# Spreading choosing steps and dense products over later stages, and moving one decoding behind a remainder, in a fused two-block layer

## The chip, the core and the metric

The kernel runs on one core of one Trainium2 chip. The metric is the device time of the whole program in microseconds (us). Five engines work side by side, each through its own program in order, and wait for each other on semaphores: TensorE (PE in the rows; PEld is its weight loads), VectorE (DVE), ScalarE (ACT), GpSimd (POOL) and SyncE (SP). GpSimd issues the gathers (indirect DMAs), SyncE the plain loads.

## The reference, cut to what matters

Two transformer blocks run one after the other on 512 tokens of width 1024. The change lies in the last part of the second, PEER: each token asks 8 heads for 16 of 16,384 single-neuron experts each, which makes 128 chosen experts for a token.

```
def peer(h, w_query, sub_keys, u_tab, v_tab):
    def block(xb):
        q = (xb @ w_query).reshape(TOKEN_BLOCK, P_HEADS, 2, P_HALF)
        s = jnp.einsum('thpk,hpnk->thpn', q, sub_keys)
        sv, si = lax.top_k(s, P_TOPK)
        cand = (sv[:, :, 0, :, None] + sv[:, :, 1, None, :]).reshape(...)
        cidx = (si[:, :, 0, :, None] * N_KEYS + si[:, :, 1, None, :]).reshape(...)
        fv, fpos = lax.top_k(cand, P_TOPK)
        eidx = jnp.take_along_axis(cidx, fpos, axis=-1)
        g = jax.nn.softmax(fv, axis=-1)
        u = u_tab[eidx]
        act = jax.nn.gelu(jnp.einsum('td,thkd->thk', xb, u), approximate=False)
        return jnp.einsum('thk,thkd->td', (g * act), v_tab[eidx])
```

The output is the sum with the residual under a last RMS norm.

## The kernel before, in words

The tokens are four blocks t = 0..3 of 128. After the dense layers of both blocks (up to about 1100 us of the span) the PEER part begins. Its query weights come as eight panels ("wq", 0..7) of 256 columns. Each panel is split into a rounded part (ScalarE, `rounded`) and a remainder (VectorE, `remainders`, L1190), and TensorE needs both before it starts on the panel (L556 to L558). Between the panels VectorE ranks one head after another of block 0 (`first_head`), and after four heads it turns places into expert numbers (`decode`, L1884 to L1919). The first 64 gathers wait for the decoding of heads 0 to 3, the other 64 for that of heads 4 to 7. A few gathered rows are used already between the panels (`FIRST_DOTS`).

Then come six stages, in the order U0, V0, U1, V1, V2, V3, each with 128 gathers of 512 KB (`gather`, L2655):

- **U0 and U1**: gather k brings, for each of the block's 128 tokens, the row of the first table that its k-th expert has, and VectorE multiplies and sums it (`dot`, L1972).
- **V0 to V3**: gather k brings the 128 rows of the second table that one token has chosen, and TensorE sums them with the weights of the token (L1145). Four tokens make one group m, so a stage has 32 groups of 16 matmul records each. ScalarE lays the weights out (`windows`, L2547). VectorE adds the result of a V stage to the residual (`finish`, L2030 to L2044).

For blocks 2 and 3 the first table is not gathered. All its 16,384 rows come as 128 plain loads of 512 KB (`ucols`, three slots, issued by SyncE as TensorE frees a slot), and TensorE multiplies each with the 256 tokens of both blocks: `dense(j)`, L1082, 16 matmul records. Afterwards 132 choosing steps `ext(s)` pick from these products those that a token has chosen: for each, TensorE spreads four tokens' key numbers (L1109, 4 records), ScalarE makes a one-hot matrix of them (L2513, L2515), TensorE multiplies with it two steps later (L1095, 8 records), and VectorE masks and sums four steps' results together (L2010, L2015, L2019). Steps 0 to 65 work on the products of the first 64 loads, steps 66 to 131 on the others. Both halves share one buffer, so dense(64) and later ones are kept only after step 65, and step 66 needs dense(127). The weights of block 2 are complete after step 99, those of block 3 after step 131.

The ranking of blocks 2, 3 and 1, in this order, is cut into 60 parts (`ranking_parts`, 20 to a block): TensorE's key scores (L1042) feed VectorE, which ranks single heads and pairs of heads and decodes twice a block. "ids" is the transposition of the expert numbers of one block (L1065, L1990).

All of this is dealt over the stages by the table `BESIDE`: an entry ("dense", 64, 124, 0, 127) means that items 64 to 123 stand evenly behind indexes 0 to 127 of the stage, an index being a gather k in a U stage and a group m in a V stage. Every engine reads the same table, so the entry sets the place of the item in each engine's program. In U1 a gather also waits for the dense products that stand 8 indexes earlier. The gathers rotate through 9 buffers in U0, 11 and then 13 from V0 on, and 17 from the 50th gather of U1 on; a gather waits until its buffer has been used.

## Time and profile before

| | us |
|---|---|
| median of 3 runs (2411.26 to 2419.2) | 2412.99 |
| profiled execution, its own time | 2416.05 |
| its span | 2414.2 |
| first gather issued | 1106.26 |
| stages by the issue of their first gather, rounded: V0, U1, V1, V2, V3 | 1370, 1591, 1825, 2017, 2211 |

Times in the rows count from the start of the span. A row of a timeline has the start, the length, engine, line, operation, output and inputs, and the count of instructions merged in it; in brackets stands the idle time before it and what ended it. A row of a window table has the window, its length, the busy time and (in brackets) the count of instructions for each engine named, then the granted TensorE clock as a share of 2.4 GHz, the mean busy share of the DMA engines, and GB/s.

### The profile page before, as it was taken

What the parts mean: (1) busy time and instruction counts of PE and PEld (TensorE: products, weight loads), DVE (VectorE), ACT (ScalarE), POOL (GpSimd) and SP (SyncE); (2) the same over time, 40 slices, a digit from 0 to 9 for tenths busy, and PEclk for the clock granted to TensorE, in tenths of its full rate; (3) what the DMA queues carried; (4) which work ended last, traced back from release to release, by engine and by line L of the source; (5) the groups of instructions that cost most, each with busy time, mean ns of one, the idle gap of its engine ahead of it and who ended that gap; (6) DMA issues with size and microseconds to landing.
All of it is one profiled execution on the core that took longest, in us unless ns stands there. A gap on an engine that the chain in (4) does not pass through costs nothing.

```text
span 2414.2 us, 31160 instructions
## 1 busy us (share of the span) xinstructions
PE 2126.6 (88%) x12429; PEld 1576.2 (65%) x12429; DVE 1308.9 (54%) x2914; ACT 643.5 (27%) x1077; POOL 885.7 (37%) x821
## 2 busy tenths in 40 slices
PE   6999889999999997899899988899898887875775
PEld 6786879889887875887788744567786454311111
DVE  3865476776456466556988775489763233100000
ACT  3335332322354333331111133421111343200000
POOL 0410000000000000002666655556766665666664
PEclk8999999999999998999999988889999898887898
DMA  4211245444212210225999998989999999999997
GB/s 178 70 36 46 112 154 198 181 174 157 89 69 105 70 53 18 88 70 185 366 415 417 406 346 312 336 309 412 413 411 419 378 343 327 348 378 368 356 374 284
DMA packets 147056, 590.01 MB, mean 244 GB/s; under 512 B 16336, under 2 KB 16464, under 8 KB 134240
## 3 DMA queue, kind: packets, MB, share of 16 engines
q0 software_dynamic: 110592, 402.70, 43.7%
q1 hardware_dynamic: 35136, 178.80, 19.7%
q10 hardware_dynamic: 1184, 6.53, 0.7%
q8 instruction: 98, 1.61, 0.3%
q14 instruction: 46, 0.38, 0.0%
HBM read 584.29 MB, written 3.67 MB: 244 GB/s over the span
## 4 chain that ended last, share of the span: by engine, by line
PE 33%; POOL 9%; DVE 8%; issue 8%; another core or an unknown queue 6%; DMA 4%; ACT 3%; SPq 0%; POOLq 0%; DVEq 0%; ACTq 0%
PE ps L1145 7%; PE ps L1082 6%; POOL big L2655 6%; PE ps L1095 5%; PE ps L556 4%; PE ps L557 4%; PE ps L558 4%; DVE cols L1972 2%; DMA big<-vtab,big 2%; DMA raw<-ucols 2%; POOL hres L2655 1%; ACT Ir L2513 1%; PE ps L1109 1%; ACT Ir L2515 1%
## 5 line engine op out<-in xcount | busy, mean ns | idle before, releaser
L1082 PE MATMUL ps<-rowb,raw 128*128 128x256 f32 x2048 | 464.4, 387 | 24.9 <-DMA raw<-ucols 22.1
L1082 PEld LDWEIGHTS ps<-rowb,raw 128*128 128x128 f32 x2048 | 391.6, 194 | 94.4 <-issue 20.8
L1145 PE MATMUL ps<-big,cols 128*32 128x512 f32 x1380 | 365.2, 692 | 77.6 <-issue 55.1
L2655 POOL DMA_INDIRECT big<-vtab,big x345 | 332.1, 963 | 190.9 <-issue 84.0
L2578 POOL TENSOR_TENSOR small<-small,cols 128x1 f32<-128x1 f32 (+3 forms) x33 | 28.9, 876 | 896.2 <-DVE small L1590 387.8
L1145 PEld LDWEIGHTS ps<-big,cols 128*32 128x32 f32 x1380 | 73.6, 121 | 254.0 <-issue 164.2
L2655 POOL DMA_INDIRECT big<-utab,cols x144 | 178.3, 1238 | 110.3 <-issue 36.6
L1972 DVE CUSTOM_DVE_ANT_0 cols<-big 128x1024 bf16<-128x1024 f32 x144 | 173.9, 1226 | 39.5 <-DMA big<-utab,cols 29.5
L1095 PE MATMUL ps<-Aj,Ir 128*128 128x64 f32 x1024 | 161.7, 301 | 27.3 <-issue 19.7
L2015 DVE TENSOR_TENSOR cols<-cols,ps 128x512 f32<-128x512 f32 x64 | 43.9, 688 | 253.0 <-remote 124.1
L2502 ACT ACTIVATE Aj<-ps 128x512 f32<-128x512 f32 x64 | 68.1, 1067 | 418.5 <-PE ps L1082 342.4
L556 PE MATMUL ps<-xhb,whb 128*128 128x512 f32 (+1 forms) x432 | 167.2, 387 | 5.9 <-ACT fbig L2356 3.0
L1095 PEld LDWEIGHTS ps<-Aj,Ir 128*128 128x128 f32 x1024 | 144.5, 214 | 38.1 <-issue 25.6
L557 PE MATMUL ps<-xhb,wlb 128*128 128x512 f32 (+1 forms) x432 | 164.1, 380 | 0.0
L558 PE MATMUL ps<-xlb,whb 128*128 128x512 f32 (+1 forms) x432 | 163.8, 379 | 0.0
L2034 DVE TENSOR_TENSOR cols<-ps,g2b 128x512 f32<-128x512 f32 x8 | 5.2, 688 | 271.3 <-remote 139.5
L2513 ACT ACTIVATE Ir<-ps,cols 128x512 f32<-128x512 f32 x128 | 87.7, 685 | 234.0 <-remote 123.8
L556 PE MATMUL ps<-whb,ah 128*128 128x256 f32 x512 | 146.0, 285 | 1.1 <-DVE al L1624 1.1
L1145 PE MATMUL ps<-hres,cols 128*32 128x512 f32 x408 | 137.1, 738 | 10.3 <-issue 5.7
L557 PE MATMUL ps<-whb,al 128*128 128x256 f32 x512 | 143.9, 281 | 0.0
L558 PE MATMUL ps<-wlb,ah 128*128 128x256 f32 x512 | 143.8, 281 | 0.0
L2109 ACT ACTIVATE whb<-raw 128x2048 fp32r<-128x2048 f32 x51 | 97.5, 1912 | 164.3 <-DMA raw<-ff 106.8
(388 smaller groups left out, 4479.7 us busy)
## 6 DMA issues: line engine op xcount, KB each, us to landing
raw<-ucols SPq DMA_DIRECT2D x128, 512.0 KB
raw<-ff SPq DMA_DIRECT2D x32, 1024.0 KB, 4.9
raw<-w SPq DMA_DIRECT2D x24, 1024.0 KB, 4.9
raw<-ada SPq DMA_DIRECT2D x24, 1024.0 KB, 4.8
raw<-wo SPq DMA_DIRECT2D x8, 1024.0 KB, 4.9
raw<-wq SPq DMA_DIRECT2D x8, 1024.0 KB, 4.8
big<-vtab,big POOLq DMA_INDIRECT x345
hres<-x SPq DMA_DIRECT2D x8, 512.0 KB, 6.4
```

What stands on the lines that cost most here:

```text
L556: e.matmul(o, lhsT=lh, rhs=rh, start=(k == 0), stop=False)
L557: e.matmul(o, lhsT=ll, rhs=rh, start=False, stop=False)
L558: ins = e.matmul(o, lhsT=lh, rhs=rl, start=False, stop=(k == n - 1))
L1082: ins = e.matmul(PS[b][:, c:c + 256], lhsT=un[j % NU][:, k, :], rhs=h2T[k // 4][:, k % 4, :], start=(k == 0), stop=(k == 7))
L1095: ins = e.matmul(PS[b][:, c:c + JC], lhsT=Ir[:, (g % 2) * 512 + q * 128:(g % 2) * 512 + (q + 1) * 128], rhs=Atd[:, 4 * g + q, :], start=Tr ...
L1145: ins = e.matmul(PS[hf][32 * j:32 * j + 32, :], lhsT=win[:, c0:c0 + 32], rhs=gs[i][:, hf * 512:(hf + 1) * 512], start=(m == 0), stop=(m == ...
L1972: e.tensor_tensor_reduce(out=junk[k % 3], in0=gs[i], in1=h2[:, t, :], scale=1.0, scalar=0.0, op0=ALU.mult, op1=ALU.add, accum_out=act[:, t ...
L2015: e.tensor_tensor(jm[n % 2], jm[n % 2], PS[(5, 7)[n % 2]][:, :], ALU.mult).then_inc(*V.mark("ex_p", (r, n)))
L2109: e.activation(hi, raw_of(n), ACT.Copy).then_inc(*A.mark("hi", u))
L2502: e.activation(Adt[:, jl:jl + 2, :], PS[2 + pair % 2][:, :].rearrange("p (j t) -> p j t", j=2), ACT.Copy).then_inc(*A.mark("dv", pair))
L2513: e.activation(one, PS[KEYS2[g % 2]][:, :], ACT.Abs, bias=pidx).then_inc(*A.mark("ex_a", r, g))
L2655: e.indirect_dma_start(gs[i], None, utab if st == "U" else vtab, bass.IndirectOffsetOnAxis(ap=idx, axis=0)).then_inc(sems[f"l_g{i}"], 16)
```

## The change

Two things are changed. In the table, the ranking of block 3 starts two heads earlier (26 parts in U0 instead of 22) and the first half of block 1's ranking ends at group 20 of V0 instead of 31. The transposition for block 2 stands behind index 126 of U0 instead of 122, and all 64 dense products of U0 stand ahead of it. The choosing steps are 50, 16, 34 and 32 in V0, U1, V1 and V2, where they were 66, 0, 54 and 12. The dense products are 64, 44 and 20 in U0, U1 and V1, where they were 64, 60 and 4.

In the panel loop, the decoding of heads 0 to 3 stands behind the remainder of panel 6 instead of ahead of it; that of heads 4 to 7 stays behind head 7.

```diff
 BESIDE = {
-    ("U", 0): [("topk", 0, 22, 10, 124), ("ids", 0, 1, 12, 12), ("ids", 1, 2, 122, 122), ("dense", 0, 64, 0, 127)],
+    ("U", 0): [("topk", 0, 26, 10, 124), ("ids", 0, 1, 12, 12), ("dense", 0, 64, 0, 125), ("ids", 1, 2, 126, 126)],
...
-    ("V", 1): [("dense", 124, 128, 0, 2), ("ext", 66, 120, 3, 31)],
+    ("V", 1): [("dense", 108, 128, 0, 11), ("ext", 66, 100, 12, 31)],
...
@@
                 if h % 2:
                     rank_pairs(0, h)
-                if h % 4 == 3:
-                    for _ in decode(0, h // 4):
-                        pass
@@
             for i in range(8):
                 panel("wq", i, last=(i == 7))
+
+                if i == 5:
+                    for _ in decode(0, 0):
+                        pass
                 if i:
                     first_head(i - 1)
...
             first_head(7)
+            for _ in decode(0, 1):
+                pass
```

The first place is VectorE's program in the panel loop. L1860 is the last operation of ranking heads 2 and 3, L1889 to L1919 are the decoding, L1190 is the remainder of panel 6, and L1844 begins head 4. Before:

```order
L1860 MAX_INDEX big<-big,cols 128x8 x2
L1889 TENSOR_SCALAR cols<-big 128x64
L1890 TENSOR_SCALAR cols<-big 128x64
L1891 TENSOR_SCALAR small<-big 128x64
L1892 TENSOR_SCALAR small<-big 128x64
L1893 TENSOR_SCALAR small<-big 128x64
L1895 COPY_PREDICATED cols<-small 128x128
```

The same place now:

```order
L1860 MAX_INDEX big<-big,cols 128x8 x2
L1190 TENSOR_TENSOR wlc<-raw,whc 128x2048
L1889 TENSOR_SCALAR cols<-big 128x64
L1890 TENSOR_SCALAR cols<-big 128x64
L1891 TENSOR_SCALAR small<-big 128x64
L1892 TENSOR_SCALAR small<-big 128x64
L1893 TENSOR_SCALAR small<-big 128x64
```

The remainder (L1190) stood behind L1919 and now stands ahead of L1889; the rest keeps its order up to head 4.

The second place is TensorE's program at the end of V0 and through U1. L1109 and L1095 are choosing steps, L1042 key scores, L1082 dense products (8 rows of this list to a product, which are 16 records of the profile), L1065 transpositions. Before:

```order
L1095 MATMUL ps<-Aj,Ir 128x64 x12
L1082 MATMUL ps<-rowb,raw 128x256 x8
L1042 MATMUL ps<-big 128x128 x2
L1082 MATMUL ps<-rowb,raw 128x256 x32
L1042 MATMUL ps<-big 128x128 x2
L1082 MATMUL ps<-rowb,raw 128x256 x24
L1042 MATMUL ps<-big 128x128 x2
L1082 MATMUL ps<-rowb,raw 128x256 x96
L1065 MATMUL ps<-cols 128x128
L1082 MATMUL ps<-rowb,raw 128x256 x320
L1065 MATMUL ps<-cols,big 128x128
```

The end of the same stretch now:

```order
L1109 MATMUL ps<-big,small 128x128 x4
L1095 MATMUL ps<-Aj,Ir 128x64 x4
L1042 MATMUL ps<-big 128x128 x2
L1109 MATMUL ps<-big,small 128x128 x4
L1095 MATMUL ps<-Aj,Ir 128x64 x4
L1109 MATMUL ps<-big,small 128x128 x4
L1095 MATMUL ps<-Aj,Ir 128x64 x12
L1082 MATMUL ps<-rowb,raw 128x256 x64
L1065 MATMUL ps<-cols 128x128
L1082 MATMUL ps<-rowb,raw 128x256 x288
L1065 MATMUL ps<-cols,big 128x128
```

The first dense product of U1 stood right behind the last choosing step of V0; now 16 choosing steps and all key scores of U1 stand ahead of it.

The third place is TensorE's program in the first groups of V1. L1145 is the weighted sum of a group. Before:

```order
L1082 MATMUL ps<-rowb,raw 128x256 x8
L1145 MATMUL ps<-big,cols 32x512 x3
L1145 MATMUL ps<-raw,cols 32x512
L1145 MATMUL ps<-big,cols 32x512 x3
L1145 MATMUL ps<-raw,cols 32x512
L1082 MATMUL ps<-rowb,raw 128x256 x16
L1145 MATMUL ps<-big,cols 32x512 x2
L1145 MATMUL ps<-B2b,cols 32x512
L1145 MATMUL ps<-big,cols 32x512 x3
L1145 MATMUL ps<-B2b,cols 32x512
L1145 MATMUL ps<-big,cols 32x512
L1109 MATMUL ps<-big,small 128x128 x4
```

The same groups now:

```order
L1082 MATMUL ps<-rowb,raw 128x256 x16
L1145 MATMUL ps<-big,cols 32x512 x3
L1145 MATMUL ps<-raw,cols 32x512
L1145 MATMUL ps<-big,cols 32x512 x3
L1145 MATMUL ps<-raw,cols 32x512
L1082 MATMUL ps<-rowb,raw 128x256 x16
L1145 MATMUL ps<-big,cols 32x512 x2
L1145 MATMUL ps<-B2b,cols 32x512
L1145 MATMUL ps<-big,cols 32x512 x3
L1145 MATMUL ps<-B2b,cols 32x512
L1145 MATMUL ps<-big,cols 32x512
L1082 MATMUL ps<-rowb,raw 128x256 x8
```

Where the choosing steps began behind the fourth group, dense products now go on, one or two behind each of the first twelve groups.

## Rows read from the trace of the kernel before

**Rows 1.** Window table of the whole core, one window a stage: PE, PEld, DVE, ACT, POOL.

```profile
1106.00:1370.00 264.00, 246.56 (x1109) 209.78 (x1109) 225.41 (x641) 33.89 (x35) 159.31 (x129) 0.97 0.94 370
1370.00:1591.00 221.00, 185.85 (x1354) 114.91 (x1357) 139.07 (x477) 89.61 (x150) 126.31 (x128) 0.86 0.89 326
1591.00:1825.00 234.00, 216.43 (x967) 181.48 (x960) 180.97 (x386) 32.40 (x33) 164.02 (x130) 0.95 1.01 405
1825.00:2017.00 192.00, 165.49 (x1136) 96.99 (x1135) 51.97 (x85) 67.85 (x115) 124.00 (x129) 0.92 0.99 374
2017.00:2211.00 194.00, 150.81 (x756) 52.20 (x758) 24.99 (x39) 26.80 (x54) 121.78 (x129) 0.83 0.94 352
2211.00:2397.00 186.00, 129.73 (x520) 29.07 (x512) 5.19 (x7) 3.25 (x15) 123.18 (x129) 0.88 0.96 367
```

**Rows 2.** Window table of L1145 alone: PE and PEld.

```profile
1370.00:1594.00 224.00, 79.54 (x512) 15.66 (x512) 0.86 0.88 322
1840.00:1868.00 28.00, 12.10 (x64) 2.39 (x64) 0.94 1.03 418
1868.00:1912.00 44.00, 18.41 (x128) 3.80 (x128) 0.92 1.00 398
1912.00:2036.00 124.00, 52.14 (x320) 11.69 (x320) 0.89 0.95 343
1496.00:1594.00 98.00, 39.18 (x256) 7.69 (x256) 0.85 0.78 278
```

**Rows 3.** Window table of L1082 alone: PE and PEld.

```profile
1106.00:1370.00 264.00, 215.96 (x960) 182.50 (x960) 0.97 0.94 370
```

**Rows 4.** Timeline of VectorE in the panel loop.

```profile
1098.34 0.20 DVE L1889 TENSOR_SCALAR cols<-big 128x64 uint32<-128x64 uint32 x1
...
1106.06 2.29 DVE L1190 TENSOR_TENSOR wlc<-raw,whc 128x2048 fp32r<-128x2048 f32 x1
...
1112.95 1.23 DVE L1972 CUSTOM_DVE_ANT_0 cols<-B2b,big 128x1024 bf16<-128x1024 f32 x1 [2.02 <-DMA B2b<-utab,cols]
...
1116.40 2.29 DVE L1190 TENSOR_TENSOR wlc<-raw,whc 128x2048 fp32r<-128x2048 f32 x1
```

**Rows 5.** Timeline of TensorE at the start of panels 5 and 6.

```profile
1091.82 0.61 PE L1042 MATMUL ps<-big 128*128 128x128 f32 x4
...
1103.40 0.61 PE L1042 MATMUL ps<-big 128*128 128x128 f32 x4
1108.50 0.76 PE L556 MATMUL ps<-xhc,whc 128*128 128x512 f32 x1 [4.50 <-DVE wlc L1190]
```

**Rows 6.** Timeline of all engines at the end of U0.

```profile
1375.04 10.53 PE L1082 MATMUL ps<-rowb,raw 128*128 128x256 f32 x48
...
1380.24 1.22 DVE L1972 CUSTOM_DVE_ANT_0 cols<-big 128x1024 bf16<-128x1024 f32 x1
...
1387.94 0.31 ACT L2557 ACTIVATE big<-big 128x128 f32<-128x128 f32 x1
```

**Rows 7.** Timeline of all engines from the end of V0 to U1.

```profile
1587.92 1.28 DVE L2015 TENSOR_TENSOR cols<-cols,ps 128x512 f32<-128x512 f32 x2
...
1591.15 1.26 POOL L2655 DMA_INDIRECT big<-utab,cols  x1 [12.07 <-DVE cols L1919]
...
1600.54 1.29 DVE L2034 TENSOR_TENSOR cols<-ps,g2b 128x512 f32<-128x512 f32 x2
...
1604.69 1.23 DVE L1972 CUSTOM_DVE_ANT_0 cols<-big 128x1024 bf16<-128x1024 f32 x1
```

**Rows 8.** Window table of DVE at the start of U1.

```profile
1600.00:1677.00 77.00, 72.98 (x209) 0.99 1.02 415
```

**Rows 9.** Window table of L1972 (DVE) in the two parts of U1.

```profile
1600.00:1677.00 77.00, 43.90 (x74) 0.99 1.02 415
1677.00:1840.00 163.00, 111.09 (x182) 0.95 1.02 412
```

**Rows 10.** Timeline of TensorE at the start of V2.

```profile
2043.56 1.07 PE L1145 MATMUL ps<-big,cols 128*32 128x512 f32 x2 [5.34 <-issue]
```

More of the change, by code:

```diff
@@ L56 @@
 BESIDE = {
-    ("U", 0): [("topk", 0, 22, 10, 124), ("ids", 0, 1, 12, 12), ("ids", 1, 2, 122, 122), ("dense", 0, 64, 0, 127)],
-    ("V", 0): [("topk", 22, 40, 0, 14), ("topk", 40, 50, 15, 31), ("ids", 2, 3, 17, 17), ("ext", 0, 32, 1, 15),
-               ("ext", 32, 66, 18, 31)],
-    ("U", 1): [("topk", 50, 60, 0, 36), ("ids", 3, 4, 44, 44), ("dense", 64, 124, 0, 127)],
-    ("V", 1): [("dense", 124, 128, 0, 2), ("ext", 66, 120, 3, 31)],
-    ("V", 2): [("ext", 120, 132, 0, 6)],
+    ("U", 0): [("topk", 0, 26, 10, 124), ("ids", 0, 1, 12, 12), ("dense", 0, 64, 0, 125), ("ids", 1, 2, 126, 126)],
+    ("V", 0): [("topk", 26, 40, 0, 12), ("topk", 40, 50, 13, 20), ("ids", 2, 3, 14, 14), ("ext", 0, 32, 1, 17),
+               ("ext", 32, 50, 18, 31)],
+    ("U", 1): [("ext", 50, 66, 0, 23), ("topk", 50, 60, 0, 36), ("ids", 3, 4, 44, 44), ("dense", 64, 108, 24, 127)],
+    ("V", 1): [("dense", 108, 128, 0, 11), ("ext", 66, 100, 12, 31)],
+    ("V", 2): [("ext", 100, 132, 0, 24)],
     ("V", 3): [],
```

## The prediction

> **What bounds the kernel now.** I read three views: first the window table, one window a stage, then the same table for single lines, then the timelines at the places where a stage hands over to the next. The first shows that the stages have different limits [rows 1]. The last one, V3, has gathers and group sums alone: 186 us for 32 groups, 5.81 us a group, with the DMA engines at 0.96 and TensorE a third idle. That is the floor of a V stage. U0 and U1 run the DMA engines at 0.94 and 1.01, move 412 GB/s where they are steady (a 0.524 MB transfer in 1.27 us) [rows 9], and keep TensorE at over 0.92: a dense product costs TensorE 215.96/60 = 3.60 us [rows 3]. V0 takes 221 us, 35 more than the floor. V1 and V2 take 192 and 194, so there are only 14 us to be had there.
>
> The second view prices what stands beside the groups [rows 2]. A group sum is 52.14/20 = 2.6 us of TensorE. In the last 20 groups of V1 a group takes 124/20 = 6.2 us with 54/29 = 1.86 choosing steps, so a step costs (6.2 - 2.6)/1.86 = 1.93 us, waits on ScalarE and VectorE included. A group reaches the floor of 5.81 us where it carries at most (5.81 - 2.6)/1.93 = 1.66 steps.
>
> A page of the Trainium skill speaks against this reading. Trace analysis, "Identifying the Most-Contended Engine", says that matmul busy time is a poor measure and weight-load busy time the better one. By weight loads V0 is at 114.91/221 = 0.52 [rows 1], and V0 would gain nothing by lighter groups. The trace sides with it only halfway: the 1.86 steps do not fill 6.2 us with matmuls, they fill them with waits between matmuls. The price per step above is taken from time, not from busy shares, and needs neither.
>
> **The change part by part.** Durations are of the profiled execution, 2416.05 us (span 2414.2), 3 us above the median of 2412.99; the sum is made against 2416 and carried over to the median.
>
> *Decoding behind the remainder.* The remainder of panel 6 ended at 1108.35 and TensorE waited 4.5 us for it [rows 4, 5]. Now it stands ahead of the decoding, starts at 1098.3 and ends at 1100.6, and panel 6 starts at once. But the decoding ends 2.3 us later, so the first gather leaves at 1108.6 instead of 1106.3 and lands at 1115.2 instead of 1112.9. VectorE stands at the first dot product until then, and the remainder of panel 7 (2.29 us at 1116.40) is queued behind two dot products: it ends near 1121 instead of 1118.7. A panel takes 11.6 us (1091.82 to 1103.40), so TensorE is ready for panel 7 at 1115.5 and waits 5 us there. The wait moves one panel on. Bounds: -4.5 us if panel 7 did not wait, +2.3 if all behind it is late; I take +1, for the late remainder is what everything behind follows.
>
> *U0.* Four more ranking parts. Ten parts cost VectorE 25 us in U1 (72.98 - 43.90 [rows 8, 9], less 4 us of `finish`), so four cost 10 us. VectorE has 264 - 225 = 39 us idle in U0 [rows 1], 22 of them behind its start, which hide them; without cover it would be +10. TensorE gains two heads' scores, 2 x 0.61 = 1.2 us [rows 5], on the path, since its last products end U0 (10.53 us for three products, up to 1385.6, against a last dot product at 1380.24 [rows 6]). New is a wait: the transposition now stands behind the 64th product, VectorE waits for it with the last dot product (1.22 us) queued behind it, and GELU (1387.94) waits for that: transposition, copies and dot product stand where ScalarE's eviction of the last product alone stood. That is 0 to 2.5 us, and I take 1.5, since the dot product alone is 1.2. U0: +3 (0 to +9).
>
> *V0.* 50 steps instead of 66. Groups 1 to 17 carry 1.88 steps instead of 2.13: -0.48 us for 17 groups, -8. Groups 18 to 31 carry 1.29, under 1.66, and go to the floor: before, the second half took 98/16 = 6.1 us a group [rows 2], so 14 x 0.3 = -4. Against this the ten ranking parts that stood behind groups 15 to 31 are pressed into 13 to 20, where VectorE then has 25 + 9 us in some 48; +2. V0: -10 (0 to -25, the latter if it reached the floor).
>
> *From V0 to U1.* Before, GpSimd waited 12.07 us for the decoding that gives U1's first numbers, and VectorE came to `finish` at 1600.54, 6 us after the last group (1594), because of choosing steps behind it [rows 7, 2]. Both go. The gathers lead anyway by 13 buffers, so the first dot product comes earlier by VectorE's 6 us and not by 12: -6 (-3 to -12).
>
> *U1.* 16 dense products leave, 16 steps come in behind the first 24 gathers, where VectorE was already full: 72.98 of 77 us [rows 8]. From the first dot product (1604.7) the three queues now need: VectorE 72 us for 37 dot products and the ranking, plus 16/4 x 3 operations of 1.28 = 15.4 us for the steps [rows 7], plus 91 x 1.22 = 111 [rows 9], 199 in all. TensorE gets its first product when VectorE has passed about three of the four sets of steps, at some 46 us, and needs 44 x 3.6 = 158 more: 204. The DMA has 32 gathers behind it by then, and 96 gathers and 41 loads ahead, 137 x 1.27 = 174: 220. The DMA still decides, for it is half idle in the opening, where no column loads can go out. With 5 us of hand-over that is 225, against 235 from 1604.7 to V1's first group at 1840: -10 (-20 if the loads overlap fully, 172 x 1.27 = 218 counted from the first gather; +3 if VectorE's opening delays each queue in turn).
>
> *V1.* The first 12 groups took 28 + 44 = 72 us [rows 2]. Now they carry 20 dense products: 12 x 2.6 + 20 x 3.6 = 103. Additivity is seen in the first four, which had four products: 28 us for 4 x 6.2. The other 20 groups carry 1.70 steps instead of 1.86: 5.9 us by the price above, 5.2 by the quicker stretch of 44 us for 8 groups; with landed gathers in 17 buffers the floor does not hold them, I take 5.6: 112 instead of 124. V1: 215 instead of 196, +19 (+8 to +30).
>
> *V1 to V2, V2.* Step 99, which completes block 2's weights, now is the last thing of V1 where it stood some ten groups earlier. Behind it come VectorE's masks and sums (3 x 1.28 us), GELU and the laying out. The hand-over was already slow, 5.34 us idle at 2043.56 [rows 10], as VectorE's steps stood ahead of `finish`: +2. In V2 the 32 steps stand 1.28 to a group, under 1.66, where 12 stood in the first seven groups; of the 8 us above the floor half should go: -4 (-8 to +4). V3 has nothing changed.
>
> Sum: 1 + 3 - 10 - 6 - 10 + 19 + 2 - 4 = -5 us. The profiled execution would be 2411, the median 2408.
>
> **Another rule weighed.** With column loads beside them the DMA engines moved 405 to 412 GB/s, alone with gathers 367 GB/s [rows 1, 9]. The Trainium skill, DMA: Bandwidth & Descriptors, "Where 436 GB/s comes from", says that for transfers between HBM and SBUF the HBM side binds at about 358. The trace does not agree in the U stages, which are above it; it does in V3. Rival A uses what the V3 row would mean if it held whenever gathers lead.
>
> **Rivals.**
>
> A. *A V stage moves 367 GB/s whatever is in it.* Then the 16 loads added to V1 cost 16 x 0.524/367 = 1.43 us each behind the gathers, 23 us, and TensorE's 31 us lie beside them, not instead; with a third of the choosing gain lost V1 is +26 instead of +19, the sum +2: 2415. For it: V2 and V3 stay at 352 and 367. Against it: V1's first 28 us, with loads in them, ran at 418 [rows 2].
>
> B. *The opening of U1 becomes the bound (slower).* VectorE is full there [rows 8]; 15.4 us more delay its dot products, so buffers, so gathers; TensorE cannot start products for 46 us; and what is missing of the DMA's work in that time is not made up because the three queues then take turns. If U1 gains nothing (0 instead of -10) and V1 costs its full 103 + 118 - 196 = +25, the sum is +11: 2424. It decides once the first product of U1 starts later than about 56 us behind the first dot product. For it: 199, 204 and 220 us lie close together. Against it: VectorE and TensorE have 20 and 16 us to spare under the DMA.
>
> C. *Steps are worth more than I count, products less.* If V0 goes to its floor for the most part (-20), and V1's products hide under gathers that TensorE would wait for, so that its first 12 groups take 92 instead of 103, the sum is -26: 2387. For it: V0 stands 35 us over the floor, and V1's rows show TensorE with 18 us idle in the last 124 us. Against it: a group is never under 2.6 us and a product never under 3.5.
>
> D. *Nothing moves.* The total work of TensorE is the same, and U1 and V1 together (431 us from first dot product to last group) give and take the same. That is within my forecast's own range and has no chance of its own.
>
> **How the numbers follow.** A measurement of this kernel tells about 0.3%, 7 us, from no change. My forecast (sum -5, its own range -14 to +6, 2399 to 2419) gets 0.48, A 0.12, B 0.2, C 0.2. Of the forecast 0.4 lies beyond -7 and hardly any beyond +7 (0.06); of A a half is beyond +7. So faster 0.48 x 0.4 + 0.2 = 0.39, slower 0.03 + 0.06 + 0.19 = 0.28, no change 0.33. The range of 8 in 10 leaves out the outer half of C and of B: 2388 to 2428.
>
> **What would show it right or wrong.** Panel 6 starting without a wait and panel 7 with one of about 5 us; the remainder of panel 7 near 1121. GpSimd's 12 us ahead of U1 gone, and `finish` right behind the last group. V0's groups 18 to 31 at about 5.8 us. The first product of U1 some 46 us behind its first dot product, U1 about 10 us shorter. The first 12 groups of V1 at about 100 us instead of 72, which is the largest single term: if they take under 90, C is nearer; if U1 is not shorter, B. V2 near 190. The prediction is wrong in its ground if V0 keeps its 221 us with 16 steps fewer, for then steps are not what holds a group.

## The result and the profile after

| | before | changed |
|---|---|---|
| median, us | 2412.99 (2407.68 to 2419.2, 7 runs) | 2426.59 (2418.78 to 2432.46, 7 runs) |
| ratio to before | | 1.0052, 95% interval 1.0032 to 1.0072 |
| profiled execution (its span), us | 2416.05 (2414.2) | 2426.49 (2424.7) |

The changed kernel is slower by half a per cent. The forecast was 5 us faster; the time lies inside the range and near rival B's 2424, on the other side of no change.

Line numbers shift by a few between the kernels: L1969, L1971 and L1968 are the dot product L1972, and L1144 is the group sum L1145.

The window table by stage, the counterpart of [rows 1]:

```profile
1106.00:1365.00 259.00, 244.84 (x1124) 209.53 (x1123) 228.38 (x680) 34.93 (x36) 158.01 (x129) 0.99 0.96 378
1365.00:1565.00 200.00, 165.59 (x1100) 88.46 (x1098) 116.07 (x408) 66.25 (x114) 126.61 (x128) 0.89 0.94 351
1565.00:1817.00 252.00, 201.98 (x935) 172.02 (x936) 194.48 (x407) 46.30 (x59) 155.65 (x130) 0.82 0.89 345
1817.00:2029.00 212.00, 186.70 (x1129) 116.39 (x1131) 36.59 (x60) 50.27 (x83) 124.15 (x129) 0.93 0.99 384
2029.00:2222.00 193.00, 156.49 (x1017) 73.70 (x1010) 43.59 (x69) 51.59 (x94) 122.05 (x129) 0.86 0.95 353
2222.00:2407.00 185.00, 129.86 (x513) 26.38 (x512) 5.19 (x7) 3.46 (x16) 123.10 (x129) 0.89 0.96 369
```

V0 lost 21 us of its length, U1 gained 18 and V1 20. U1 is the stage to look at: its DMA share fell from 1.01 to 0.89 and its granted clock from 0.95 to 0.82. A count from one piece of visible work to the next tells more than the issue of gathers. The lines give the lengths of the pieces in the two traces, their difference, and the forecast:

| piece | before | changed | difference | forecast |
|---|---|---|---|---|
| up to the panels (panel 5's key scores, 1091.8 and 1089.1) | | | -2.8 | |
| from there to U0's 7th dot product | 63.9 | 62.2 | -1.7 | +1 |
| to V0's first group (1389.6 and 1381.4) | 233.9 | 230.1 | -3.8 | +3 |
| V0, first to last group | 204.7 | 193.3 | -11.4 | -10 |
| V0's last group to U1's first dot product | 10.4 | 16.9 | +6.5 | -6 |
| U1, first to last dot product | 231.3 | 242.1 | +10.8 | -10 |
| V1, its hand-over included | 199.9 | 215.8 | +15.9 | +19 |
| V1 to V2, and V2 | 181.1 | 181.0 | -0.1 | -2 |
| the rest | | | -3 | 0 |

Two terms cost time where a gain was forecast: the hand-over to U1 was off by 12 us and U1 by 21. The terms of the decoding and of U0 missed the other way, by 10 us together; V0 and V1 came near their forecast.

The opening of U1, 87 us from its first dot product, and the rest of it (PE, PEld, DVE, ACT, POOL, then clock, DMA share, GB/s), the counterpart of [rows 8, 9]:

```profile
1592.00:1679.00 87.00, 60.63 (x288) 54.85 (x287) 83.18 (x226) 18.85 (x28) 44.83 (x38) 0.68 0.73 259
1679.00:1834.00 155.00, 132.27 (x576) 111.26 (x576) 111.91 (x184) 21.74 (x21) 111.91 (x91) 0.94 1.01 406
```

VectorE is busy for 83.2 of 87 us, and the DMA engines move 259 GB/s. The 87 us from the first dot product of before:

```profile
1605.00:1692.00 87.00, 81.84 (x362) 69.15 (x361) 82.58 (x226) 11.75 (x12) 58.92 (x48) 0.96 1.02 412
```

VectorE was as busy before, but it did 48 dot products in that time and now does 37. The size of the loss can be estimated from these rows: (412 - 259) x 87 us are 13.3 MB, 25.4 transfers of 0.524 MB. Sixteen of them are the loads that left U1 and need not be made up; 9.4 must be, and 9.4 x 1.27 = 12 us, against 10.8 measured.

GpSimd's timeline shows why the DMA engines had less to do:

```profile
1593.08 1.68 POOL L2658 DMA_INDIRECT big<-utab,cols  x1 [10.00 <-DVE big L1969]
...
1606.93 1.68 POOL L2658 DMA_INDIRECT hres<-utab,cols  x1 [3.22 <-DVE big L1969]
...
1620.56 1.68 POOL L2658 DMA_INDIRECT big<-utab,cols  x1 [4.55 <-DVE big L1969]
...
1674.70 1.68 POOL L2658 DMA_INDIRECT hres<-utab,cols  x1 [6.93 <-DVE big L1969]
```

The gathers leave in bursts, and ahead of a burst GpSimd waits for a dot product (L1969) to free a buffer: when the first dot product began, 13 gathers of U1 had been issued, as many as there are buffers. TensorE in the same stretch, the idle time in brackets:

```profile
1584.64 0.61 PE L1109 MATMUL ps<-big,small 128*128 128x128 bf16 x4 [7.57 <-issue]
...
1603.65 1.94 PE L1095 MATMUL ps<-Aj,Ir 128*128 128x64 f32 x8 [8.59 <-DVE cols L2018]
...
1631.72 1.94 PE L1095 MATMUL ps<-Aj,Ir 128*128 128x64 f32 x8 [7.30 <-DVE cols L2018]
...
1639.06 19.69 PE L1082 MATMUL ps<-rowb,raw 128*128 128x256 f32 x80
...
1677.50 0.47 PE L1065 MATMUL ps<-cols 128*128 128x128 f32 x1 [7.42 <-DVE cols L1919]
```

TensorE's steps wait for VectorE's masks, the first product starts 47.5 us behind the first dot product, and in the middle of the products the transposition for block 1 waits 7.4 us for VectorE's last decoding. A step's product of 8 records takes 1.94 us here and 1.06 in V0: TensorE's granted clock was at its lower level, 1.2 GHz, from its stop of 7.57 us to the first products (0.50 in the window 1579 to 1643, 41 of 64 us busy), so that 0.68 is the mean of the 87 us, where it was 0.96 before.

The changed kernel's panel loop, VectorE and then TensorE, beside [rows 4, 5]:

```profile
1095.57 2.29 DVE L1190 TENSOR_TENSOR wlc<-raw,whc 128x2048 fp32r<-128x2048 f32 x1
1097.97 0.20 DVE L1889 TENSOR_SCALAR cols<-big 128x64 uint32<-128x64 uint32 x1
...
1110.55 1.23 DVE L1969 CUSTOM_DVE_ANT_0 cols<-B2b,big 128x1024 bf16<-128x1024 f32 x1 [2.40 <-DMA B2b<-utab,cols]
...
1114.12 2.29 DVE L1190 TENSOR_TENSOR wlc<-raw,whc 128x2048 fp32r<-128x2048 f32 x1
```

```profile
1112.21 0.61 PE L1042 MATMUL ps<-big 128*128 128x128 f32 x4
1116.55 0.47 PE L556 MATMUL ps<-xhc,whc 128*128 128x512 f32 x1 [3.73 <-DVE wlc L1190]
```

Panel 6 starts without a wait and panel 7 with one of 3.73 us. The remainder of panel 7 ends 27.4 us behind panel 5's key scores, 26.9 before. Against panel 5's key scores the first gather left 2.4 us later, as worked out, but the first dot product began only 0.4 us later: it followed the issue of the gather by 4.7 us instead of 6.7. That holds in every trace: 4.4 to 4.7 us in the eleven with the decoding moved, 6.5 to 6.8 in the three without. Why the two differ was not tried.

The end of U0, beside [rows 6]:

```profile
1377.50 0.45 PE L1065 MATMUL ps<-cols 128*128 128x128 f32 x1 [4.09 <-DVE big L1993]
...
1378.08 1.23 DVE L1969 CUSTOM_DVE_ANT_0 cols<-big 128x1024 bf16<-128x1024 f32 x1
...
1379.57 0.31 ACT L2560 ACTIVATE big<-big 128x128 f32<-128x128 f32 x1
```

TensorE is through with the products before the last dot product, and GELU (L2560, L2557 before) starts 1.5 us behind the start of that; before, it was 7.7, since ScalarE first had to evict TensorE's last products.

### The profile page after: what moved, and what is told of

It is laid out like the page before. It is cut to its first block, busy times and chain, and to the rows that moved or that the text cites. A ratio compares the mean times of both kernels' runs of the same rounds, so it can differ in the third digit from the quotient of the medians.

```text
span 2424.7 us, 31147 instructions
## 1 busy us (share of the span) xinstructions
PE 2120.4 (87%) x12429; PEld 1582.0 (65%) x12429; DVE 1308.2 (54%) x2914; ACT 642.6 (27%) x1077; POOL 876.9 (36%) x821
## 4 chain that ended last, share of the span: by engine, by line
PE 26%; DVE 14%; POOL 10%; issue 7%; DMA 6%; another core or an unknown queue 5%; ACT 2%; DVEq 0%; POOLq 0%; ACTq 0%
POOL big L2658 6%; PE ps L1145 6%; DVE cols L1969 6%; PE ps L556 4%; PE ps L558 4%; PE ps L557 4%; PE ps L1082 3%; PE ps L1095 3%; DMA big<-utab,cols 2%; POOL hres L2658 2%; DMA big<-vtab,big 2%; DMA B2b<-utab,cols 1%; POOL raw L2658 1%; PE ps L932 1%
## 5 line engine op out<-in xcount | busy, mean ns | idle before, releaser
L1082 PE MATMUL ps<-rowb,raw 128*128 128x256 f32 x2048 | 462.5, 386 | 22.2 <-DMA raw<-ucols 19.4
L1082 PEld LDWEIGHTS ps<-rowb,raw 128*128 128x128 f32 x2048 | 389.7, 193 | 96.9 <-issue 20.7
L1145 PE MATMUL ps<-big,cols 128*32 128x512 f32 x1380 | 355.1, 684 | 70.1 <-issue 51.7
L2658 POOL DMA_INDIRECT big<-vtab,big x345 | 331.8, 962 | 199.9 <-issue 91.8
L1145 PEld LDWEIGHTS ps<-big,cols 128*32 128x32 f32 x1380 | 69.5, 119 | 232.3 <-issue 165.9
L1095 PE MATMUL ps<-Aj,Ir 128*128 128x64 f32 x1024 | 170.3, 313 | 48.4 <-issue 22.8
L2658 POOL DMA_INDIRECT big<-utab,cols x144 | 170.2, 1182 | 100.8 <-issue 38.5
L1969 DVE CUSTOM_DVE_ANT_0 cols<-big 128x1024 bf16<-128x1024 f32 x144 | 173.6, 1226 | 35.3 <-DMA big<-utab,cols 25.5
L1095 PEld LDWEIGHTS ps<-Aj,Ir 128*128 128x128 f32 x1024 | 154.9, 227 | 56.5 <-issue 47.3
L1190 DVE TENSOR_TENSOR wlb<-raw,whb 128x2048 fp32r<-128x2048 f32 x51 | 116.9, 2293 | 40.8 <-ACT whb L2112 37.8
L1145 PE MATMUL ps<-hres,cols 128*32 128x512 f32 x408 | 128.2, 686 | 10.1 <-DMA hres<-vtab,big 6.3
```

The source lines that it names most:

```text
L1082: ins = e.matmul(PS[b][:, c:c + 256], lhsT=un[j % NU][:, k, :], rhs=h2T[k // 4][:, k % 4, :], start=(k == 0), stop=(k == 7))
L1095: ins = e.matmul(PS[b][:, c:c + JC], lhsT=Ir[:, (g % 2) * 512 + q * 128:(g % 2) * 512 + (q + 1) * 128], rhs=Atd[:, 4 * g + q, :], start=Tr ...
L1145: ins = e.matmul(PS[hf][32 * j:32 * j + 32, :], lhsT=win[:, c0:c0 + 32], rhs=gs[i][:, hf * 512:(hf + 1) * 512], start=(m == 0), stop=(m == ...
L1190: e.tensor_tensor(lo, raw_of(n), hi.bitcast(F32), ALU.subtract).then_inc(*V.mark("lo", u))
L1969: e.tensor_tensor_reduce(out=junk[k % 3], in0=gs[i], in1=h2[:, t, :], scale=1.0, scalar=0.0, op0=ALU.mult, op1=ALU.add, accum_out=act[:, t ...
L2658: e.indirect_dma_start(gs[i], None, utab if st == "U" else vtab, bass.IndirectOffsetOnAxis(ap=idx, axis=0)).then_inc(sems[f"l_g{i}"], 16)
```

## The experiments

They ran on three chips. On that of e1 to e4 the kernel before takes 2311 us, on that of e9 to e12 it takes 2310, and on that of e5 to e8 it takes 2417, near the 2413 of the result. "The quicker chip" below means the first two, which are taken for alike; "the slower chip" means the third and that of the result, of which the record doesn't say whether they are one. Ratios are to before on the same chip. The kernel before was not profiled on a quicker chip; the decoding alone stands for it there. "Dots" is the time from U1's first to its last dot product.

| kernel | ratio, 95% interval | V0 groups | dots | V1 groups |
|---|---|---|---|---|
| decoding alone (e1) | 0.9985, 0.9977 to 0.9994 | 168.0 | 235.2 | 162.4 |
| table alone (e2) | 1.0086, 1.0073 to 1.0099 | 170.1 | 240.8 | 186.2 |
| steps back (e3) | 1.0041, 1.0028 to 1.0054 | 174.9 | 227.0 | 185.2 |
| ranking alone (e4) | 1.0006, 0.9996 to 1.0015 | 173.9 | 234.2 | 162.9 |
| light products (e9) | 1.0053, 1.0040 to 1.0066 | 167.0 | 240.6 | 180.9 |
| spread (e10) | 0.9992, 0.9982 to 1.0002 | 174.2 | 215.6 | 185.8 |
| end of U0 (e11) | 0.9983, 0.9974 to 0.9991 | 173.4 | 234.1 | 162.0 |
| store behind (e12) | 0.9968, 0.9955 to 0.9981 | 175.5 | 233.0 | 163.2 |
| changed again (e5), slower chip | 1.0081, 1.0057 to 1.0104 | 198.6 | 242.7 | 213.2 |
| small masks (e6), slower chip | 1.0038, 1.0020 to 1.0057 | 195.6 | 229.9 | 213.5 |
| ids late (e7), slower chip | 1.0075, 1.0052 to 1.0098 | 199.9 | 240.4 | 214.4 |
| products back (e8), slower chip | 1.0153, 1.0124 to 1.0182 | 196.1 | 270.8 | 191.6 |

**Decoding alone, table alone, changed again.** The first has the panel loop of the change and the table of before, the second the other way round, the third is the changed kernel.

```diff
             for i in range(8):
                 panel("wq", i, last=(i == 7))
+                if i == 5:
+                    for _ in decode(0, 0):
+                        pass
...
```

> The kernel before, with the decoding of heads 0 to 3 moved behind the remainder of panel 6, and nothing else. Theory T (from the two traces: the last eviction of panel 7 came about 1.6 us earlier against the panel's start): 1.5 us less, 2411. Rival (the sum on record): the late remainder of panel 7 costs 1 us more, 2414. In the trace T wants panel 6 to start without a wait and the first dot product of U0 at the same distance from panel 5 as in the changed kernel.

> The changed table with the panel loop of before. Theory T: all of the loss is the table's, 2428 (15 us over before; the changed kernel plus 1.5). Rival: the loss belongs to both parts together (a later start of U0 meets the fuller opening of U1 otherwise), and the table alone is within 5 us of before, 2418.

> The changed kernel once more, beside the experiments that follow, for the first experiments ran where a group of V3 took 5.0 us instead of 5.8. Theory T (the loss is transfers and VectorE's work, which the clock changes little): ratio to before 1.004 to 1.009. Rival (the loss is TensorE's half clock in some stages alone): within 0.3% of before where the clock is 0.96 or more.

The decoding alone took 2307.56 against 2311.23 us, the table alone 2331.49. TensorE's panels in the first of them:

```profile
1092.53 0.61 PE L1041 MATMUL ps<-big 128*128 128x128 f32 x4
...
1120.04 0.47 PE L555 MATMUL ps<-xhc,whc 128*128 128x512 f32 x1 [3.74 <-DVE wlc L1189]
1132.83 0.60 PE L1041 MATMUL ps<-big 128*128 128x128 f32 x4
```

and in the second:

```profile
1091.77 0.61 PE L1041 MATMUL ps<-big 128*128 128x128 f32 x4
...
1108.44 0.77 PE L555 MATMUL ps<-xhc,whc 128*128 128x512 f32 x1 [4.49 <-DVE wlc L1189]
...
1133.61 0.61 PE L1041 MATMUL ps<-big 128*128 128x128 f32 x4
```

From panel 5's key scores to those behind the last panel it takes 40.3 us instead of 41.8: the edit is worth 1.5 us there, as theory T had it. The medians are 3.7 us apart, with an interval of 1.4 to 5.3, so what it gives beyond 1.5 is not shown. The whole loss is the table's. The two ratios together give 1.007 for the changed kernel, which on the slower chip had 1.0052 and, once more, 1.0081: the loss does not hang on the chip, as T had it. The span's mean granted clock is 0.93 on the slower chip and 0.96 in the table alone.

**Ranking alone.**

```diff
-    ("U", 0): [("topk", 0, 22, 10, 124), ...
-    ("V", 0): [("topk", 22, 40, 0, 14), ("topk", 40, 50, 15, 31), ("ids", 2, 3, 17, 17), ...
+    ("U", 0): [("topk", 0, 26, 10, 124), ...
+    ("V", 0): [("topk", 26, 40, 0, 12), ("topk", 40, 50, 13, 20), ("ids", 2, 3, 14, 14), ...
```

> The kernel before with the ranking's part of the change alone: 26 parts in U0, parts 40 to 49 behind groups 13 to 20 of V0, the transposition of block 3 behind group 14; steps and products as before. Theory T: GpSimd's wait of 12 us ahead of U1 goes, U1 starts 3 to 6 us earlier, U0 pays 2: about 2410. Rival: VectorE still has choosing steps behind the last group and the gathers lead by 13 buffers anyway, so nothing is won there and U0 pays 3: 2416.

Nothing is won, and V0's groups take 5.9 us more than in the decoding alone. The first dot product follows the last group by 10.4 us with the ranking moved and by 10.2 without: GpSimd's wait ahead of U1 (7.25 us in the decoding alone) is gone, but the buffers had covered it, and VectorE's steps behind the last group stood there still. The rival was right.

**Steps back.** The changed kernel with its 16 steps of U1 again in V0. The products stay.

```diff
-               ("ext", 32, 50, 18, 31)],
-    ("U", 1): [("ext", 50, 66, 0, 23), ("topk", 50, 60, 0, 36), ("ids", 3, 4, 44, 44), ("dense", 64, 108, 24, 127)],
+               ("ext", 32, 66, 18, 31)],
+    ("U", 1): [("topk", 50, 60, 0, 36), ("ids", 3, 4, 44, 44), ("dense", 64, 108, 24, 127)],
```

> The changed kernel with the 16 choosing steps of U1 put back into V0 (66 steps there, groups 18 to 31 as before), the dense products staying at 44 behind indexes 24 to 127 of U1 and 20 in V1. Theory T (the steps keep VectorE full in U1's opening, dot products come late, buffers and so gathers come late, the DMA engines starve): first to last dot product of U1 takes 220 to 228 us instead of 242, V0 takes 8 us more, in all about 2417. Rival R (it is the late begin of the products, not VectorE, that lengthens U1): first to last dot product stays at 238 to 242, V0 takes 8 more, 2433.

The dots took 227.0 instead of the table's 240.8: the steps in U1's opening cost 13.8 us. In V0 the same 16 steps cost 4.8 us (174.9 against 170.1), where T had asked 8. T was right in the mechanism. But 227.0 is only 8 below the 235.2 of the kernel with all 60 loads in U1, where 16 loads of 1.27 us are 20.

**Spread.** As steps back, with the 44 products of U1 spread behind indexes 0 to 127.

```diff
-    ("U", 1): [..., ("dense", 64, 108, 24, 127)],
+    ("U", 1): [..., ("dense", 64, 108, 0, 127)],
```

> The kernel of the steps put back into V0 (e3), with its 44 dense products of U1 behind indexes 0 to 127 instead of 24 to 127. Theory T (a load taken out of U1 pays 1.27 us only if the opening still carries its share of loads; with a late begin the DMA engines starve there): first to last dot product of U1 5 to 9 us shorter than the 227 of e3, the kernel about 6 below it, ratio to before 1.000 to 1.003. Rival (U1 is bound by the total of its transfers and not by their place): as e3, 1.004.

The dots took 215.6 us, 11.4 less than with the late begin, where T had asked 5 to 9. The opening's 87 us in both, steps back first and spread second:

```profile
1566.00:1653.00 87.00, 46.92 (x188) 38.99 (x189) 82.44 (x227) 5.34 (x6) 54.00 (x46) 0.72 0.87 316
```

```profile
1567.00:1654.00 87.00, 65.69 (x292) 55.38 (x291) 82.58 (x226) 9.82 (x10) 58.33 (x52) 0.88 0.97 380
```

64 GB/s over 87 us are 10.6 transfers, 13.5 us by 1.27. So four kernels of the quicker chips give U1 in single steps, each from one trace: 235.2, less 19.6 for 16 loads taken out evenly, plus 11.4 for the products' late begin, plus 13.8 for the steps, is 240.8. The first of these steps also has U0's end and the ranking moved, which alone change the dots by about 1 us (234.1 and 234.2).

**Small masks.** The masks, products and sums of U1's 16 steps cover 64 columns instead of 512, so that the kernel leaves out part of the choosing.

```diff
-                iot = iotaf[:, r * JC:(r + 1) * JC]. ... .to_broadcast([128, 8, JC])
-                by8 = lambda x: x.rearrange("p (c j) -> p c j", j=JC)
+                J = 8 if r == 0 and g >= 53 else JC
+                iot = iotaf[:, r * JC:r * JC + J]. ... .to_broadcast([128, 8, J])
+                by8 = lambda x: x.rearrange("p (c j) -> p c j", j=J)
...
```

> The changed kernel, but VectorE's mask, product and sum of the 16 steps of U1 read and write 64 columns instead of 512; that part of the choosing is left out. All waits stay. Theory T (VectorE's 15 us in U1's opening delay dot products, so gathers): first to last dot product of U1 8 to 14 us shorter, the kernel 8 to 12 us below the changed one. Rival R1 (TensorE holds the opening: its steps run at half clock and the products start late whatever VectorE does): 0 to 3 us.

The dots took 12.8 us less than in the changed kernel on the same chip, and the median 9.1 us less, as T asked. A pair of masks in the changed kernel, and in this one:

```profile
1601.61 1.29 DVE L2013 TENSOR_TENSOR cols<-cols,big 128x512 f32<-128x512 f32 x2
```

```profile
1610.67 0.36 DVE L2014 TENSOR_TENSOR cols<-cols,big 128x64 f32<-128x64 f32 x2
```

Three such pairs for each four steps make 15 us of VectorE's time, and 11 are gone. TensorE's clock in the opening is hardly above the changed kernel's 0.68, and its first product still comes 40.9 us behind the first dot product, 6.6 us earlier than there:

```profile
1601.00:1688.00 87.00, 70.92 (x335) 64.27 (x333) 82.18 (x243) 21.42 (x31) 55.89 (x44) 0.71 0.85 300
```

So VectorE's time for the steps is nearly all of their 13.8 us. What TensorE's lower level costs was not measured, for both kernels have it.

**Ids late.**

```diff
-    ("U", 1): [..., ("ids", 3, 4, 44, 44), ...
+    ("U", 1): [..., ("ids", 3, 4, 60, 60), ...
```

> The changed kernel with the transposition for block 1 behind index 60 of U1 instead of 44, so that TensorE does not stand 7 to 9 us for VectorE's last decoding among the dense products. Theory T (gathers and loads share DMA engines that have been starved by then, a part of the stop is made up): 1 to 4 us below the changed kernel. Rival R2 (this wait is what makes U1 longer): 7 to 9 us below it.

The dots are 2.3 us shorter and the median is 0.5 lower, less than the runs can tell. But the edit did not take TensorE's stop away:

```profile
1687.05 0.31 ACT L2487 ACTIVATE cols<-cols 128x128 f32<-128x128 f32 x1 [21.88 <-DVE cols L1951]
```

```profile
1688.33 23.29 PE L1081 MATMUL ps<-rowb,raw 128*128 128x256 f32 x96 [9.21 <-ACT Aj L2504]
```

ScalarE's part in block 1's ranking (L2487) stands ahead of its evictions of the products (L2504) and waits for VectorE's operations behind the decoding. So TensorE stands 9.2 us for an evicted product at the place where it stood 7.4 us for the transposition. The run tells nothing of what the stop costs: R2 stays untested.

**Products back.**

```diff
-    ("U", 1): [..., ("dense", 64, 108, 24, 127)],
-    ("V", 1): [("dense", 108, 128, 0, 11), ("ext", 66, 100, 12, 31)],
+    ("U", 1): [..., ("dense", 64, 124, 24, 127)],
+    ("V", 1): [("dense", 124, 128, 0, 2), ("ext", 66, 100, 12, 31)],
```

> The changed kernel with 60 dense products in U1, still behind indexes 24 to 127, and 4 in V1 as before. Theory T (a load costs its transfer, about 1.3 us, in either stage, for both keep the DMA engines full behind their openings): U1 12 to 20 us longer, V1 16 to 25 us shorter, in all -8 to +2 against the changed kernel. Rival (the sum on record: 3.6 us of TensorE for each product that starts 46 us late): TensorE needs 46 + 60 x 3.6 = 262 us, U1 20 us longer, and V1 only 14 shorter since gathers hide some of its products: +6 or more.

This is 14.8 us slower than the changed kernel: the dots are 28 us longer, V1's groups 22 shorter, and another 14 us lie between the last dot product and V1's first group, for TensorE comes last. The rival was right and T wrong: 60 products behind a late begin are TensorE's queue, 3.6 us each, with 16 us of waits between them.

```profile
1590.00:1677.00 87.00, 66.59 (x322) 60.56 (x321) 83.11 (x227) 19.75 (x30) 44.43 (x38) 0.71 0.75 266
1677.00:1861.00 184.00, 171.47 (x758) 146.91 (x759) 112.41 (x185) 26.46 (x26) 104.61 (x84) 0.95 0.95 372
```

TensorE is busy for 171 of the last 184 us while the DMA engines fall to 372 GB/s. With steps in the opening, moving the 16 products out of U1 saved time; the two halves of the table belong together.

**Light products.** The last 16 dense products take 2 of their 16 matmul records each, so that the kernel leaves out most of their sums; all loads stay.

```diff
-                for k in range(8):
+                for k in range(8 if j < 112 else 1):
```

> The changed kernel, but the last 16 dense products, all in V1, take 2 of their 16 matmul records; the rest of them is left out. Their loads and all waits stay. The first 12 groups of V1 take 96 to 97 us in the changed kernel and 63 to 72 before. Theory P (TensorE's time for the products, 3.6 us each, is the price of V1): 12 groups in 78 to 84 us, the kernel 10 to 16 us below the changed one. Rival A (the DMA engines' time for 16 loads more, 1.27 us each, is the price): 90 to 97 us, 0 to 5 below.

The changed kernel was not run on this chip, so the table alone, which has the same V1, stands for it. V1 in the table alone and then in this kernel, the first 12 groups and the other 20:

```profile
1805.00:1902.00 97.00, 96.70 (x512) 65.51 (x512) 1.29 (x2) 10.07 (x16) 46.91 (x50) 0.97 1.02 416
1902.00:1992.00 90.00, 88.53 (x697) 46.18 (x696) 27.73 (x43) 42.78 (x74) 66.54 (x70) 1.00 0.99 395
```

```profile
1797.00:1877.00 80.00, 66.93 (x287) 25.27 (x288) 1.12 (x2) 9.74 (x16) 44.35 (x48) 0.93 1.03 419
1877.00:1978.00 101.00, 98.75 (x692) 47.38 (x692) 27.73 (x43) 42.74 (x74) 74.30 (x79) 1.00 1.03 419
```

The first 12 groups fell by 17 us, as theory P had it, but the other 20 took 11 more, and V1 as a whole is only 5 us shorter. Without TensorE's share the DMA engines run at 419 GB/s to the end. The decoding alone, without the 16 loads but with 20 choosing steps more in V1, has 63 and 99 us:

```profile
1807.00:1870.00 63.00, 62.81 (x432) 35.22 (x430) 12.28 (x19) 21.31 (x37) 44.87 (x48) 0.97 1.03 419
1870.00:1969.00 99.00, 98.40 (x757) 52.77 (x757) 36.10 (x57) 48.44 (x85) 75.24 (x79) 1.00 1.03 419
```

At 419 GB/s from end to end the stage takes 162 us, and 181 with 16 loads more: 19 us, and 16 x 1.27 is 20. Of V1's 24 us the transfers are 19 and TensorE's work is 5. The price of the whole stage is that of this run's rival A, that of its beginning is TensorE's.

**End of U0, and store behind.** Both have the decoding moved and, of the table, U0's end alone; the second also moves SyncE's store of block 0 behind the last load.

```diff
-    ("U", 0): [("topk", 0, 22, 10, 124), ("ids", 0, 1, 12, 12), ("ids", 1, 2, 122, 122), ("dense", 0, 64, 0, 127)],
+    ("U", 0): [("topk", 0, 22, 10, 124), ("ids", 0, 1, 12, 12), ("dense", 0, 64, 0, 125), ("ids", 1, 2, 126, 126)],
```

```diff
-                if j == 100:
-                    e.wait_ge(sems["l_park"], 48)
-                    back(0)
-            for t in range(1, NT):
+            e.wait_ge(sems["l_park"], 48)
+            for t in range(NT):
                 back(t)
```

> The kernel before with the decoding moved (e1) and, of the table, only the end of U0: all 64 dense products behind indexes 0 to 125, the transposition for block 2 behind 126. Theory T (TensorE's last products, not VectorE, ended U0): the first group of V0 4 to 7 us earlier than in e1 against the start of U0, 2 to 4 us of it left at the end, since V0's gathers are paced by the DMA engines: ratio 0.997. Rival (the sum on record: the transposition, its copies and the last dot product come onto the path, 1.5 us): 0.999 or 1.000.

> As e11, and SyncE stores block 0's result and reads block 1's rows back behind the last of the 128 loads instead of behind load 100, where TensorE stands 8.5 us in U1 because SyncE issues no load meanwhile. Theory T (the DMA engines are the limit there and work on gathers meanwhile, so the stop is made up): within 2 us of e11. Rival (TensorE's stop is lost for good, for the gathers wait for products): 4 to 8 us below e11, ratio 0.994.

V0's first group came 272.6 us behind U0's first gather instead of 280.7 in the decoding alone, more than T asked, and V0's groups gave 5.4 us of it back: 0.9983 beside 0.9985 is no difference. With the store behind, TensorE's stop is gone, and at the end of U1 it waits longer instead; first the end of U0 alone, then with the store behind:

```profile
1708.79 30.11 PE L1081 MATMUL ps<-rowb,raw 128*128 128x256 f32 x128 [8.46 <-DMA raw<-ucols]
...
1799.19 0.47 PE L1064 MATMUL ps<-cols,big 128*128 128x128 f32 x1 [5.58 <-DVE big L2079]
```

```profile
1800.31 0.47 PE L1064 MATMUL ps<-cols,big 128*128 128x128 f32 x1 [14.66 <-DVE big L2079]
```

The dots took 233.0 against 234.1: in U1 the stop was made up, as T says. The medians are 3.3 us apart (2305.83 and 2302.56), between T's 2 and the rival's 4, with intervals that overlap, so whether the move is worth something stays open. It is the quickest kernel of this study and quicker than both: 0.9968 of before.

## Why the prediction was wrong

**The step that failed** is U1, "The DMA still decides, for it is half idle in the opening" with 220 us, -10. It measured 242.1, +10.8. Its own numbers up to 46 us were right: the first product came at 47.5, and the 32nd gather was issued 4 us ahead of it. Wrong was that the DMA engines would run full from then on. GpSimd may lead VectorE's dot products by 13 buffers only, VectorE was full until its steps and ranking were over at 87 us, and over these 87 us the engines moved 259 GB/s. Three queues were each summed on their own and the longest taken, where one feeds the other. The experiments price it: the 16 loads taken out are worth the 20 us that the sum took, the late begin of the products costs 11.4, the steps 13.8 (12.8 by the masks alone), and the sum had 10 for both. The late begin works through the loads that the opening lacks (316 against 380 GB/s), the steps through the buffers. Rival B has this mechanism. That its 2424 is near the measured time is partly luck: it had U1 at 0 and V1 at +25, and the other terms off by amounts that cancel. The point that it named, a first product later than 56 us, was not reached and was no criterion.

**From V0 to U1**, -6 forecast, +6.5 measured. VectorE's steps behind the last group did not go: two steps of group 31 stand there still, and `finish` takes 4.2 us before the first dot product. On the quicker chip the table alone shows 8.6 us from last group to first dot product, against 10.2: -1.6. The other 8 us are about TensorE's stop of 7.6 us at 1584.64, below. Such a stop is there in all five traces of the changed table's V0 on the slower chip, with 7.6 to 9.0 us in four and 2.2 in the fifth, and not in the one of before, so on that chip it may belong to the change.

**V0**, -10 forecast, -11.4 measured, on the slower chip. The sum behind it does not hold. It takes 0.48 us off each of groups 1 to 17, but groups 16 and 17 carried no step before, so by its own prices that is 6 us and not 8. And its 1.93 us a step does not fit its own row of V0's second half: 34 steps in 16 groups of 6.1 us are 1.65 a step. On the quicker chip 16 steps cost 4.8 us, and from the first gather to V0's last group the table alone takes 446.6 us where the decoding alone takes 448.8 (469 and 488 in the result's two traces): the price per step was that of one chip, and that -10 came out is in part luck.

**V1**, +19 forecast, +17 measured in its groups (+24 on the quicker chip). The first 12 groups took 97 us, where 103 was forecast. The size was right, but the cause, TensorE's work, holds for these groups alone; on the quicker chip, where it was tried, the stage as a whole pays for transfers.

**Decoding**, +1 forecast, -1.7 measured, and **U0**, +3 forecast, -3.8. In the first the time from the issue of the first gather to its use was carried over as a constant of 6.6 us, and it was 4.7. In the second TensorE's 10.5 us of last products were read in the row, yet what ends them earlier was not counted: with all 64 by index 125 they were off the path, and the transposition, whose 1.5 us were counted, lay beside the last dot products.

**V2**, -4 forecast, -0.3 measured in its groups: it carries 32 steps laid out evenly where it had 12 in its first groups, and takes the same time.

The sum took the loads' move from U1 to V1 as two terms of different kinds, transfers in U1 and TensorE's work in V1. Both stages keep the DMA engines full where nothing starves them; 16 loads cost 20 us in the one and 19 in the other, plus TensorE's 5.

## What to carry to other kernels

Where a stage's transfers wait for buffers that a second engine frees, work added to that engine in the opening lowers the transfer rate until it has caught up; the loss can be estimated by the missing bytes of that stretch, read from its GB/s, and not by the difference between queues summed by themselves. The estimate is good to a few us: 12 for 10.8 and 13.5 for 11.4 here, but 9 for the 5.6 us between the decoding alone and the table alone (418 and 277 GB/s in their openings). A load moved between two stages that both keep the DMA engines full is worth nothing, as long as TensorE is not the longer queue in one of them, as it was in products back. A price per item taken from one chip's trace should be taken a second time where another chip shows other rates. And an experiment that moves a wait should be read for whether the wait is gone: in ids late it had gone to the next operation.

## What the runs showed of the hardware

The chips differ in the V stages. Up to the first gather the traces agree within some us, and U0 takes 257 to 264 us on both. But V3, with gathers and group sums alone, takes 186 us on the slower chip [rows 1] and 161 on the quicker, here in the decoding alone:

```profile
2119.00:2280.00 161.00, 139.23 (x511) 25.07 (x510) 5.18 (x7) 3.46 (x16) 122.39 (x129) 1.00 1.03 420
```

So gathers alone move 420 GB/s. On the slower chip they do so too, between dips; its GB/s in slices of 5 us, 2200 to 2400 of the changed kernel:

```profile
GB/s 389 292 413 419 338 330 419 420 420 211 272 297 406 420 420 298 354 292 389 419 419 419 419 415 287 360 410 420 420 292 320 371 417 420 419 242 338 395 421 420
```

The decoding alone has no such dip in V3 (414 to 423). So the 367 on which rival A rested is the mean of two states and no limit of the DMA engines. The Trainium skill, DMA: Bandwidth & Descriptors, "Where 436 GB/s comes from", says that for transfers between HBM and SBUF the HBM side binds at about 358 GB/s. The 367 lay near it, but the 420 of gathers alone is above it on both kinds of chip.

On the slower chip TensorE stops now and then in V stages with nothing late that the profile shows: for up to 2.2 us within V3, 7.6 us at the end of V0, and 16.6 us ahead of V3 in the kernel before (1.4 in the decoding alone). These are, at the end of V0 of the changed kernel, TensorE's last record of a step's product, and ScalarE behind its wait:

```profile
1576.01 1.06 PE L1095 MATMUL ps<-Aj,Ir 128*128 128x64 f32 x8
```

```profile
1583.90 0.69 ACT L2516 ACTIVATE Ir<-ps,cols 128x512 f32<-128x512 f32 x1 [9.34 <-remote]
```

The records end at 1577.1, and ScalarE goes on 7 us later. The same place in the changed kernel's second profile:

```profile
1589.58 0.69 ACT L2516 ACTIVATE Ir<-ps,cols 128x512 f32<-128x512 f32 x1 [10.10 <-remote]
```

ScalarE's wait is 10 us again. On the quicker chip the table alone has no stop there. What makes TensorE stop, what makes the dips, and whether the two are one thing, was not tried and stays open.
